# Columns of the weight products read alternately from the two halves of a row, in runs of 16

## The reference

```python
def _swiglu(h, w_gate, w_up, w_down):
    return (jax.nn.silu(h @ w_gate) * (h @ w_up)) @ w_down

for i in range(DEPTH):                       # first stack, DEPTH = 2
    fx = _swiglu(_pre(hx, ...), ffn_w_gate[i, 0], ffn_w_up[i, 0], ffn_w_down[i, 0])
    fc = _swiglu(_pre(hc, ...), the same three weights)
    ...                                      # windowed attention (i = 0), differential attention (i = 1)
    fx = _swiglu(_pre(hx, ...), ffn_w_gate[i, 1], ffn_w_up[i, 1], ffn_w_down[i, 1])
    if with_ctx_out:                         # i = 0 only
        fc = _swiglu(_pre(hc, ...), the same three weights)
for l in range(DEPTH):                       # second stack
    x = x + 0.5 * _swiglu_2(h, ffn_pre_w_gate[l], ffn_pre_w_up[l], ffn_pre_w_down[l])
    x = x + mixer(h)                         # retention and dilated attention (l = 0), gated linear attention (l = 1)
    x = x + 0.5 * _swiglu_2(h, ffn_post_w_gate[l], ffn_post_w_up[l], ffn_post_w_down[l])
```

## Time and profile before

| | |
|---|---|
| time, median of 3 runs | 2813.97 us (2809.7 to 2837.8) |
| the profiled execution | 2824.21 us, of which the span is 2822.4 us |
| TensorE matmul busy | 2740.4 us (97%), 17468 instructions |
| TensorE weight load busy | 2420.4 us (86%) |
| VectorE busy | 1768.1 us (63%) |
| ScalarE busy | 1206.6 us (43%) |
| granted TensorE clock, mean | 0.991 of full |

### The profile page before, as it was taken

One profiled execution on the slowest core, in us unless ns is written; L12 is line 12 of the kernel. 1 busy time (PEld: TensorE's weight loads), 2 busy tenths in 40 slices (PEclk: granted clock), 3 DMA queues, 4 the chain that ended last, 5 costly groups with the idle time before them and its releaser, 6 DMA issues.

```text
span 2822.4 us, 45969 instructions
## 1 busy us (share of the span) xinstructions
PE 2740.4 (97%) x17468; PEld 2420.4 (86%) x17468; DVE 1768.1 (63%) x2690; ACT 1206.6 (43%) x1808; POOL 200.2 (7%) x246
## 2 busy tenths in 40 slices
PE   7999999999999999999998999999989999999998
PEld 5888886678888888888875999999879999988998
DVE  5977344847874287732548655667666666667665
ACT  4322223833222243322326555654446556544563
POOL 0100011010100100001100101002000000000001
PEclk9999999999999999999999999999989999999999
DMA  8666323025664346633330565666426566653564
GB/s 307 209 197 186 95 88 90 2 75 170 209 191 122 113 155 192 187 90 98 102 104 16 161 183 181 191 187 218 121 90 183 182 181 192 181 167 97 174 189 137
DMA packets 118687, 424.31 MB, mean 150 GB/s; under 512 B 13280, under 2 KB 14320, under 8 KB 117408
## 3 DMA queue, kind: packets, MB, share of 16 engines
q1 hardware_dynamic: 98528, 353.41, 40.5%
q0 software_dynamic: 18992, 68.09, 8.0%
q10 hardware_dynamic: 1040, 1.05, 0.1%
HBM read 421.45 MB, written 1.05 MB: 150 GB/s over the span
## 4 chain that ended last, share of the span: by engine, by line
PE 88%; DVE 6%; ACT 2%; issue 2%; DMA 1%; SPq 0%; DVEq 0%; ACTq 0%
PE bank L741 28%; PE bank L742 28%; PE bank L743 28%; DVE WL L1579 1%; ACT WH L1242 1%; DMA f_nat<-in_ada_n 1%; DVE rstd L1775 1%; DVE g_max L1878 1%; DVE d_small L1940 1%; PE bank L874 1%; PE bank L982 0%; PE bank L959 0%; DVE g_p L1898 0%; DVE tn L1785 0%; DVE x_all L1795 0%
## 5 line engine op out<-in xcount | busy, mean ns | idle before, releaser
L741 PE MATMUL bank<-x_all,WH 128*128 128x256 f32 (+1 forms) x3776 | 1217.8, 322 | 23.4 <-DVE x_all L1795 6.2
L742 PE MATMUL bank<-x_all,WH 128*128 128x256 f32 (+1 forms) x3776 | 1205.5, 319 | 0.0
L743 PE MATMUL bank<-x_all,WL 128*128 128x256 f32 (+1 forms) x3776 | 1205.2, 319 | 0.0
L1579 DVE TENSOR_TENSOR WL<-raw,WH 128x1024 fp32r<-128x1024 f32 (+1 forms) x664 | 806.9, 1218 | 626.2 <-ACT WH L1242 623.0
L1242 ACT ACTIVATE WH<-raw 128x1024 fp32r<-128x1024 f32 (+1 forms) x664 | 682.3, 1035 | 796.5 <-PE bank L743 782.3
L741 PEld LDWEIGHTS bank<-x_all,WH 128*128 128x128 f32 x3776 | 716.6, 190 | 86.0 <-issue 12.1
L742 PEld LDWEIGHTS bank<-x_all,WH 128*128 128x128 f32 x3776 | 715.9, 190 | 54.7 <-issue 3.1
L743 PEld LDWEIGHTS bank<-x_all,WL 128*128 128x128 f32 x3776 | 713.8, 189 | 52.8
L743 PE MATMUL bank<-h_all,WL 128*128 128x256 f32 (+1 forms) x1408 | 450.9, 320 | 0.0
L741 PE MATMUL bank<-h_all,WH 128*128 128x256 f32 (+1 forms) x1408 | 450.9, 320 | 0.0
L742 PE MATMUL bank<-h_all,WH 128*128 128x256 f32 (+1 forms) x1408 | 450.9, 320 | 0.0
(11 more groups left out here) (318 smaller groups left out, 1620.6 us busy)
## 6 DMA issues: line engine op xcount, KB each, us to landing
a_rows<-in_ada_t POOLq DMA_DIRECT2D x124, 512.0 KB, 4.1
raw<-in_ffn_w_gate SPq DMA_DIRECT2D x88, 512.0 KB, 3.6
raw<-in_ffn_w_up SPq DMA_DIRECT2D x88, 512.0 KB, 4.3
raw<-in_ffn_w_down SPq DMA_DIRECT2D x64, 512.0 KB, 3.6
raw<-in_ffn_pre_w_gate SPq DMA_DIRECT2D x44, 512.0 KB, 3.6
raw<-in_ffn_pre_w_up SPq DMA_DIRECT2D x44, 512.0 KB, 4.3
raw<-in_ffn_post_w_gate SPq DMA_DIRECT2D x44, 512.0 KB, 3.6
raw<-in_ffn_post_w_up SPq DMA_DIRECT2D x44, 512.0 KB, 4.4
```

The source lines that it names most:

```text
L741: nc.tensor.matmul(o, WH[:, j % 4, k, :], high, start=start, stop=False)
L742: nc.tensor.matmul(o, WH[:, j % 4, k, :], low, start=False, stop=False)
L743: return nc.tensor.matmul(o, WL[:, j % 4, k, :], high, start=False, stop=stop)
L1579: nc.vector.tensor_tensor(WL[:, b, 0:d, :], raw[:, b, 0:d, :], WH[:, b, 0:d, :].bitcast(F32), ALU.subtract).then_inc(split_done, 1)
```

## The change

In `three`, all of the moving operands (high, low) and the output go through `in_turn`: the row of 512 (256) columns is cut into two halves, and the instruction takes 16 columns from the first half, 16 from the second, the next 16 from the first, and so on. The output bank is addressed in the same way, so every result stands where it stood. The same change of tables moves the views: offsets of 0, 16, 32 and 48 words (and 8 for the last hidden layer) in place of 0, 112 and 368. The number and the order of the instructions and the waits of all engines stay as they were.

```diff
-        NORM_X = (0, 0, 0, 0, 0, 112, 112, 112, 112, 112, 112, 112, 0)
-        MIX_X = (0, 112, 112, 112)
-        FFN_H = (0, 0, 0, 368, 368, 368, 368, 368)
+        NORM_X = (0, 16, 32, 48, 0, 16, 32, 48, 48, 0, 16, 16, 0)
+        MIX_X = (32, 48, 48, 16)
+        FFN_H = (16, 32, 48, 0, 16, 32, 48, 8)
...
+            def in_turn(ap):
+
+                return ap.rearrange("p (h l n) -> p l h n", h=2, n=16)
+
             def three(g, j, b, k, start, stop):
                 high, low = g.rhs(k + (DT * (b % 3) if g.down else 0), g.t)
                 o = (bank[4 + (b // 3 if g.down else b) % 2] if g.kind == "res" else bank[b])[:, 0:g.t]
+                o, high, low = (in_turn(ap) for ap in (o, high, low))
                 nc.tensor.matmul(o, WH[:, j % 4, k, :], high, start=start, stop=False)
                 nc.tensor.matmul(o, WH[:, j % 4, k, :], low, start=False, stop=False)
                 return nc.tensor.matmul(o, WL[:, j % 4, k, :], high, start=False, stop=stop)
```

## The result

The changed kernel takes 2931.7 us (median of 4 runs, 2930.3 to 2933.3) against 2819.2 us of the kernel before in the same comparison (4 runs): a ratio on record of 1.0375, 95% interval 1.0341 to 1.0409. (The ratios given here are those on record; they aren't always the quotient of the two medians, which is 1.040 here.) The profiled execution has a span of 2930.0 us, 107.6 more than before.

A forecast was written before the change was run, and what follows sets the result against it. TensorE's products in `three` were taken to bound the kernel; gains of 45 us at 512 columns and 17 us at 256 sum to 62, so 2814 - 62 = 2752 us. Its own range was 2712 to 2790, the overall range 2710 to 2950.

The forecast's parts named there:

- What bounds the kernel: TensorE is busy 97% of the span; time is the number of products in `three` times the distance between starts.
- The alternate runs: In `three`, moving address and weight load keep their distance: 512 columns go to 216 ns, 256 columns to 113.3.
- the row at 1.2 GHz: Products of 256 columns at the halved clock take 213.3 ns, nothing over; taken as showing equal paces are good.
- `ident` against `ident`: Plain matmuls reading `ident` as weights and moving operand start 112 ns apart; taken as showing equal paces are good.
- The idea behind it: In `three`, moving columns meet the next weight load, causing the excess over floors of 216 and 112 ns; 101 us together.
- The offsets: They set the distance to the weights; stages at 0 gain nothing, leaving 62 us, up to 101 if offset doesn't matter.
- The jumps: 323,000 jumps in the products of `three`, 0 to 3 ns each by the nearest rows; taken as 0, upper end 970 us.
- What is late next: VectorE in the gate and up stage would be at 86%, still covered; weights would rise to 211 GB/s.
- Rival 2: Slower by jumps in `three`: each costs one column, 0.42 ns, 135 us; 2949 us, or 2887 with relief; chance 0.26.
- The test that the prediction named: In `three`, twice as many ns over at 512 columns as at 256 speaks for slower by jumps, 31 to 15.
- Rival 1: No change: TensorE loses a column in each 16, 226.7 ns being 17 for 16; 0 +- 15 us, 2814; chance 0.23.
- Rival 3: Slower by a lock: equal-pace streams hold each other, some 107 ns more at offset 0, over 300 us; chance 0.06.

The follow-up runs named there:

- experiment 9: Kernel before, offsets 0, reading side, four pieces: jumping in plain order modulo 256 bytes; runs twice; plain, halves (both 64-column WL): 228.2, 240.0, 230.3, 240.0 ns.
- experiment 6: Plain order, new offsets, both weight buffers 48 words further on: 228.9, 232.4, 233.3, 226.7 ns at 0, 16, 32, 48 words, 512 columns.
- experiment 1: New offsets alone, columns in plain order, against the kernel before: 2854.8 us, ratio 1.0103.
- 2: Alternate order alone, with the old offsets, against the kernel before: 2932.3 us, ratio 1.0386.
- 5: Kernel before, moving operand alone alternating, second run half a row less 0, 16, 32, 48 words away: 240.0, 240.2, 240.5, 240.0 ns at 512 columns.
- experiment 4: Kernel before, four pieces: plain, reading side alone in turn, writing side alone, both: 228.2, 240.0, 228.2, 240.0 ns at 512 columns.
- experiment 3: Changed kernel with old offsets, runs of 8, 32, 64 and 128 columns in the four pieces: 243.4, 236.7, 226.9, 226.6 ns.
- experiment 12: Kernel before, at 256 columns the first product of each second piece takes runs of 16 over eighths of the row: 2804.8 us, ratio 0.9942.

## Why the prediction was wrong

*What bounds the kernel* held. The instructions, the chain and the waits are the same, and the time moved by what the distance moved.

*The step that failed is the first of the change, "The alternate runs".* It said that the low address then goes at the pace of the weights, that the two keep their distance through the whole load, and that equal paces are good, so that 226.7 goes down to 216 and 117.8 to 113.3. The first half is true of the addresses. The second is wrong: 240 and 120 ns came in place of 216 and 113.3, and no steady stage of any run went below 226.7 or 113.3. Experiment 9 shows it without a far half: reading each run twice, at half the pace, costs the same 13.3 ns. The two rows it leaned on were of another kind. In the row at 1.2 GHz and in `ident` against `ident` the moving side takes one word in 0.83 ns. In turn it still takes two words in that time, and only the line address is slow. A row that has the same ratio of addresses but half the rate of words was no evidence for this one.

*The idea behind it was half right.* That moving columns and weights meet, and that it depends on their distance, is shown by experiment 6, where shifting the weights by 48 words turns the whole table. But that part is 0 to 6.7 ns. The larger part of the excess in plain order (13.3 ns at 512 columns at the best distance) was taken for the same thing, and no run shows that; with half of the weights to load it didn't shrink (third piece of experiment 9). Since the loss in turn stays when only 64 weights load (experiment 9) and at any distance (1, 2 and 5), reading in turn costs the moving stream something that neither changes.

*The offsets.* The step had 0 as bad and the others as good in the new order. In the new order they do nothing (2931.7 against 2932.3 us with the old table). In the plain order, 0 is the best of 0, 16, 32 and 48 at 512 columns and the worst at 256, and the new table by itself costs 1.0%.

*The jumps* were taken at 0, and at 512 columns they are free on both sides (experiments 4 and 9). *What is late next* wasn't put to the test: all distances grew, and with them the time that covers VectorE and the weights.

*The rivals.* Rival 2, slower by the jumps, gave 2949 with one column lost a jump and no relief, and the time is 2932. The size is nearly right, since 13.3 ns over 31 jumps is 0.43, but for a reason that isn't the one: experiment 9 has the jumps without the loss, and experiment 3 has twice and half the jumps without twice and half of it. The test that the prediction named, twice the loss at 512 columns as at 256, is met (13.3 against 6.7 over the pace of 113.3), and it didn't tell a jump from a line in a bad order. Rival 1's reading of 226.7 as 17 for 16 now has 240 as 18 for 16 beside it, but it isn't a law: 232.1, 236.6 and 243.4 of other orders are no whole number of columns lost in each 16. Its conclusion, that the order of addresses would not touch the pace, is wrong. Rival 3, one stream held by the other, asked for stages far out, and there are none.

*What stays open.* Of the orders measured at 512 columns and offset 0, those whose lines stand at 0, 1, 2, 3 modulo four cost 226.7 to 229.0 (plain, runs of 64 and 128, second half first, the jumping one). Others cost from 232.1 (quarters) over 233.4 (backward), 236.6 (swapped, and runs of 32) and 239.1 (eighths) to 240.0 (halves, sixteenths, each run twice) and 243.4 (runs of 8, half a line each). No simple rule was found that gives these sizes, and what inside TensorE or SBUF makes them wasn't shown.

## What to carry to other kernels

Where float32r products bound a kernel, read the distance from start to start by stage before anything else: it shows in 0.1 ns what an edit of addresses does, and one run can carry four variants in the four pieces of a round. Variants side by side touch each other, though: the plain piece read 226.7 to 229.0 by its neighbours, so differences under 2 ns want a run of their own. Let the moving operand run upward in plain order, start it on a 64-byte line, and choose its distance to the weights modulo 256 bytes for each column count apart (here 0 at 512 columns; at 256 columns 192 bytes is the best of those tried, and even there the pace can be 117.8 in place of 113.3). And when a row is taken as evidence for a pace, see that it has the same rate of words, not the same ratio of addresses.

## What the runs showed that was not expected

- At 256 columns the same instructions at the same addresses have two steady paces, 113.3 and 117.8 ns. They hold one for hundreds of products; a wait can change it, or something that the trace doesn't show (1778 us of the kernel before, where no distance is over 122 ns). Offset 16 has both paces too. In experiment 1 it ran at 113.3 in the fourth mixer's output and at 117.8 in the eighth ffn right behind:

```profile
2635.00:2643.00 8.00, 8.00 (x73) 1.00 0.58 171
...
2680.00:2740.00 60.00, 60.00 (x512) 1.00 0.66 193
```

So a single stage of 256 columns doesn't tell what a place costs. One product in another order sets it to 113.3; done in each second piece, it makes the kernel 0.6% faster than the one before (experiment 12). Why the paces exist wasn't shown.
- The distance of moving columns and weights modulo 256 bytes costs 0 to 6.7 ns a product, and the distance that is best at 512 columns is the worst of the four at 256 (experiments 1 and 6).
- A pattern on the output side in runs of 16 float32 costs nothing at 512 columns (experiment 4), and neither do 31 jumps on the reading side, if the lines come in the order 0, 1, 2, 3 modulo 256 bytes (experiment 9, first piece).
